# Adding the squares of the new h over its eight tiles on GpSimd, in place of TensorE products in four bands

## The reference

```
def rmsnorm(x, g):
    y = xf * lax.rsqrt(jnp.mean(xf * xf, axis=-1, keepdims=True) + RMS_EPS)
def post_add(h, y, g_post, gate, weight):
    return h + weight * gate[:, None, :] * rmsnorm(y, g_post)

per layer:  h = post_add(h, swiglu(pre_mod(h, ...)), ...)    feed-forward network a
            h = post_add(h, mixer(pre_mod(h, ...)), ...)     attention and gating
            h = post_add(h, swiglu(pre_mod(h, ...)), ...)    feed-forward network b
```

## Time and profile before

| | us |
|---|---|
| median of 3 runs | 2848.84 (2848.16 to 2849.9) |
| profiled execution, its own time | 2847.8 |
| its span | 2846.0 |
| PE busy | 2783.9 (98%) |
| DVE busy | 1298.3 (46%) |
| ACT busy | 971.0 (34%) |
| POOL busy | 111.2 (4%) |

### The profile page before, as it was taken

One profiled execution on the slowest core, in us unless ns is written; L12 is line 12 of the kernel. 1 busy time (PEld: TensorE's weight loads), 2 busy tenths in 40 slices (PEclk: granted clock), 3 DMA queues, 4 the chain that ended last, 5 costly groups with the idle time before them and its releaser, 6 DMA issues.

```text
span 2846.0 us, 49978 instructions
## 1 busy us (share of the span) xinstructions
PE 2783.9 (98%) x21654; PEld 2628.9 (92%) x21654; DVE 1298.3 (46%) x2533; ACT 971.0 (34%) x1821; POOL 111.2 (4%) x210
## 2 busy tenths in 40 slices
PE   7999999999999999999999999999999999999997
PEld 6999999878999989999999999998889999999997
DVE  3444424655544464443264443256555445544423
ACT  4222324444422452222252222244443225422322
POOL 0000000010000000000000000001100000000000
PEclk9999999999999999999999999999999999999999
DMA  6444532333222234432224444323322222222221
GB/s 245 149 148 149 172 121 93 110 123 98 92 82 82 82 104 149 148 134 88 88 86 152 149 149 165 112 100 116 122 96 68 82 82 75 82 82 82 86 87 66
DMA packets 90186, 319.82 MB, mean 112 GB/s; under 512 B 11360, under 2 KB 14464, under 8 KB 89776
## 3 DMA queue, kind: packets, MB, share of 16 engines
q1 hardware_dynamic: 64048, 222.50, 23.4%
q0 software_dynamic: 25920, 94.14, 9.7%
HBM read 305.70 MB, written 11.55 MB: 111 GB/s over the span
## 4 chain that ended last, share of the span: by engine, by line
PE 85%; DVE 7%; ACT 3%; DVEq 2%; issue 2%; DMA 1%; SPq 0%; ACTq 0%
PE ps L668 77%; PE ps L782 2%; PE ps L1013 2%; PE ps L1059 1%; DVE h L1671 1%; ACT w_hi L1162 1%; DVE x_lo L1678 1%; PE ps L1035 1%; DVEq L1670 1%; DVE z L1669 1%; PE ps L677 1%; DMA w_raw<-in_f 1%; ACT sig L1498 1%; ACT x_hi L1254 1%; DVEq L2017 1%
## 5 line engine op out<-in xcount | busy, mean ns | idle before, releaser
L668 PE MATMUL ps<-x_hi,w_hi 128*128 128x290 f32 (+1 forms) x4256 | 973.8, 304 | 22.7 <-DVE x_lo L1678 13.6
L668 PE MATMUL ps<-x_lo,w_hi 128*128 128x290 f32 (+1 forms) x4256 | 935.4, 295 | 0.0
L668 PE MATMUL ps<-x_hi,w_lo 128*128 128x290 f32 (+1 forms) x4256 | 934.8, 295 | 0.0
L668 PEld LDWEIGHTS ps<-x_hi,w_hi 128*128 128x128 f32 x4256 | 686.7, 189 | 95.1 <-issue 65.3
L668 PEld LDWEIGHTS ps<-x_lo,w_hi 128*128 128x128 f32 x4256 | 701.1, 190 | 0.3
L668 PEld LDWEIGHTS ps<-x_hi,w_lo 128*128 128x128 f32 x4256 | 692.7, 189 | 0.0
L1553 DVE TENSOR_TENSOR w_lo<-w_raw,w_hi 128x1024 fp32r<-128x1024 f32 x386 | 468.8, 1222 | 254.2 <-ACT w_hi L1162 251.9
L1162 ACT CAST w_hi<-w_raw 128x1024 fp32r<-128x1024 f32 x386 | 392.9, 1047 | 77.3 <-DMA w_raw<-in_f 77.3
L668 PE MATMUL ps<-hid_hi,w_hi 128*128 128x288 f32 x1344 | 300.8, 295 | 1.8 <-DVE c_col L1610 1.8
L668 PE MATMUL ps<-hid_hi,w_lo 128*128 128x288 f32 x1344 | 300.7, 295 | 0.0
L668 PE MATMUL ps<-hid_lo,w_hi 128*128 128x288 f32 x1344 | 298.7, 293 | 0.0
(11 more groups left out here) (214 smaller groups left out, 2391.8 us busy)
## 6 DMA issues: line engine op xcount, KB each, us to landing
w_raw<-in_f SPq DMA_DIRECT2D x260, 512.0 KB, 3.5
ada_w<-in_ada POOLq DMA_DIRECT2D x128, 512.0 KB, 5.7
w_raw<-in_gate SPq DMA_DIRECT2D x64, 512.0 KB, 3.5
w_raw<-in_tri SPq DMA_DIRECT2D x42, 512.0 KB, 3.5
ada_first<-in_ada SPq DMA_DIRECT2D x4, 2048.0 KB, 17.7
w_raw<-in_wout SPq DMA_DIRECT2D x16, 512.0 KB, 3.4
decay_s<-f_scratch POOLq DMA_DIRECT2D x16, 272.0 KB, 6.0
decay_p<-f_scratch POOLq DMA_DIRECT2D x8, 512.0 KB, 5.9
```

The costliest lines, as they stand in the source:

```text
L668: r = mm(ps[:, 2 * out + b, 0:width], w, xx[:, cols(b)], start=first and n == 0, stop=last and n == 2)
```

## The change

The products in bands and the copy by ACT go away, with their two semaphores. In their place GpSimd adds tiles 1 to 7 of the squares into tile 0, half 0 first, one instruction for a tile and a half: 14 in a boundary, 70 in all. Each waits for its square and for the addition before it. `sum_of_h` keeps its place and now waits for the fourteenth addition. On GpSimd's list the additions of the first boundary of a layer stand behind the loads of network a and ahead of the mixer's DMAs, those of the second ahead of the loads of network b, and those of the third behind them.

```
@@ first_group, on PE
-            some(0, (0, 1, 2), (3, 4, 5))
-            if not first:
-                bands_of_h(*j, 0, 0)
-            some(0, (0, 1, 2), (6, 7))
+            some(0, (0, 1, 2), (3, 4, 5, 6, 7))
...
                 some(1, (0, 1, 2), (k,))
-                if not first and k in LATE_SUMS:
-                    bands_of_h(*j, *LATE_SUMS[k])
@@ sum_of_h, on PE
-            pe.wait_ge(bands_taken.sem, bands_taken.done(l, j))
+            pe.wait_ge(sq_h_added.sem, sq_h_added.done(l, (j + 1) * ADDS - 1))
@@ first_raw and before_pairs, on ACT
-                if s == 1 and (l or ab == "b"):
-                    take_bands(*((l, 1) if ab == "b" else (l - 1, 2)))
...
-                if s == 0:
-                    take_bands(l, 0)
@@ on GpSimd
+        def add_squares(l, j):
+            n = j * ADDS
+            for b in BOTH:
+                total = sq_h[:, 0, columns(b)]
+                for k in range(1, KD):
+                    pool.wait_ge(sq_h_ready.sem, sq_h_ready.done(l, x_index(j, b, k)))
+                    if k > 1:
+                        pool.wait_ge(sq_h_added.sem, sq_h_added.done(l, n - 1))
+                    nc.gpsimd.tensor_tensor(total, total, sq_h[:, k, columns(b)], ALU.add
+                                            ).then_inc(sq_h_added.sem, 1)
+                    n += 1
...
             ada_loads(l, "a")
+            add_squares(l, 0)
             mixer_outputs(l)
...
             stage(l, B_PAIRS + 1, 1, 3, None)
+            add_squares(l, 1)
             ada_loads(l, "b")
+            if l < DEPTH - 1:
+                add_squares(l, 2)
```

More of the change, by code:

```diff
@@ L127 @@
 BAND = P // BANDS
-LATE_SUMS = {1: (0, BANDS), 5: (1, 0), 7: (1, BANDS)}
+ADDS = 2 * (KD - 1)
 BANDS_AT = 2
@@ L487, in build_program @@
     sq_h_ready = S("sq_h_ready", 6 * KD)
-    bands_ready = S("bands_ready", 3)
-    bands_taken = S("bands_taken", 3)
+    sq_h_added = S("sq_h_added", 3 * ADDS)
     sum_h_ready = S("sum_h_ready", 3)
@@ L1210, in first_raw @@
                 r.then_inc(acc_free[s].sem if s < 2 else alt_taken.sem, 1)
-                if s == 1 and (l or ab == "b"):
-                    take_bands(*((l, 1) if ab == "b" else (l - 1, 2)))
-        def take_bands(l, j):
-            act.wait_ge(bands_ready.sem, bands_ready.done(l, j))
-            A(two(sq_h[:, 0, :]), pair[3], ACT.Copy, scale=1.0 / BAND).then_inc(bands_taken.sem, 1)
         def estimate_h(l, j):
```

## The result

| | us |
|---|---|
| before, median of 4 runs | 2848.97 (2848.16 to 2849.9) |
| after, median of 4 runs | 2877.39 (2874.58 to 2879.9) |
| ratio | 1.0099, 95% interval 1.0086 to 1.0111 |
| profiled execution after, its own time and span | 2879.9, 2878.1 |

The change makes the kernel 28.4 us slower; 34.6 us was forecast. The profiled execution is the longest of the four, so its rows show 32 us more than before in place of 28.

The account below looks back on a forecast made before the run. PE, busy 98% of the span, was taken as the bound, waiting for DVE at boundaries. Profiled 2847.8 + 36.0 - 1.4 = 2882.4, with the median 1.0 higher: 2883.4 us; the forecast's own range 2862 to 2897.

Parts of the forecast that it names:

- DVE's chain sets a boundary, and PE moves with it: At both tiles 6 PE already waits for DVE's low part of x, so 7.20 us a boundary delays everything after.
- Each addition holds DVE up for its whole length, 0.65 us: At boundaries, GpSimd additions stall DVE instructions reading two SBUF tiles; 0.65 us each, bounds 0.456 and 1.18; forecast's chance 0.52.
- Rival 1: At the boundaries GpSimd and DVE don't disturb each other; only the 1.4 us saving remains, 2847.4 us; chance 0.28.
- Eleven of the fourteen count: Per boundary, eleven additions delay DVE fully, the third mostly fits DVE's 0.60 us gap, half 1's last two cost nothing.
- The removal saves 1.4 us: Only the last of four band groups costs PE: 0.5 us saved at two boundaries, 0.12 us at three.
- The new wait and the moved loads cost nothing: `sum_of_h` has 1.9 us in hand at worst; network b's first two loads stay hidden with 9 us in hand.
- The sum: Whole kernel: 36.0 us for the hold on DVE less 1.4 us for the removed bands.
- Rival 2: At boundaries POOL stands still instead of DVE, making PE 4.4 us late at `sum_of_h`; +22 us, 2871; chance 0.15.

Follow-up runs that it names:

- experiment 2: Kernel before, bands and copy kept, plus 14 GpSimd additions of 128x288 at each boundary that nothing reads: 2873.53 us, ratio 1.0085.
- experiment 7, third run: Kernel before plus 144 GpSimd additions of 128x256 in the feed-forward networks, two a step, waiting for ACT's hid_hi: 2849.95 against 2849.36 us, ratio 1.0001.
- experiment 3: Kernel before plus 14 GpSimd memsets of 288 columns at each boundary, with the additions' waits and signals: 2849.57 us, ratio 1.0001.
- experiment 1: Changed kernel without its 70 GpSimd additions, so the sum of squares lacks tiles 1 to 7: 2848.42 against 2849.49 us, ratio 0.9996.
- the filler: Changed kernel plus unused PE products ahead of waits for x_lo, 22 in half 0, 4 and 10 in half 1: 2873.63 us, ratio 1.0085.

## Why the prediction was right, point by point

- *DVE's chain sets a boundary, and PE moves with it*: right, and shown. The same additions cost 24.0 us there (experiment 2), and 19.5 us of DVE's time cost nothing where DVE waits for PE (experiment 7, third run).
- *Each addition holds DVE up for its whole length, 0.65 us*: the right mechanism, both numbers off. An addition takes 0.79 us at the shortest and 1.10 us on average. Those that hold DVE up do so for 0.52 us on average, and over all 70 it is 0.49 us. Rival 1, no disturbance, falls with experiments 2 and 3. The Trainium skill's page "SBUF — State Buffer", section "Who interferes with whom", names as colliding a DVE instruction with two SBUF inputs and a GpSimd instruction that reads. Additions and copies, memsets, and DVE's instruction on PSUM behave as it says. It adds that the one that comes later stands still until the other is done, and the trace agrees: z, which ran first, kept its 0.75 us while the addition ended 0.66 us after it, and h, which came later, ended some 0.62 us after the addition. The hold is less than the addition's length since the turn is shorter: 0.66 us of 0.79, and DVE's h, 0.76 us by itself, needs only 0.61 us more once the addition has ended, so about 0.15 us of it had passed while it stood waiting. That the 0.65 us charged is almost the turn is chance: it was taken from ACT's pass, as the length of an addition.
- *Eleven of the fourteen count*: right. Twelve additions end ahead of tile 6 of half 1, and eleven of them hold DVE up, by 0.36 to 0.61 us; one, the second and not the third, runs in DVE's gap of 0.61 us. The eleven make 5.45 us, and the gap of 0.23 us ahead of x_lo is used up: 5.2 us, where PE's delay is 5.14. So the mis-sized term is the hold, 0.50 us in place of 0.65: 5 x 5.16 = 25.8 us in place of the 36.0 worked out.
- *The removal saves 1.4 us*: 1.1 us by experiment 1, which is within its interval, and 1.2 us by its rows.
- *The new wait and the moved loads cost nothing*: right. The fourteenth addition ends 2.7 us ahead of the sum, and memsets in the same place of POOL's list cost nothing (experiment 3).
- *Missing from the prediction*: the clock. The longer waits let PE's clock fall to its lower level, and part of the products after them run at half the rate. In the changed kernel's profiled execution the five fourth chunks are 5.93, 5.75, 6.63, 5.96 and 5.97 us late, 30.2 us together. With the filler, at a clock of 1.00, they are 4.72, 5.09, 5.17, 4.71 and 5.10 us late, 24.8 us. So the clock costs 5.4 us in this execution, the longest of four. Of the medians it is about 4 us: 28.4 us for the changed kernel and 24.1 for the filler kernel, each against its own runs of the kernel before.
- *The sum*: 36.0 - 1.4 = 34.6 us was forecast. Shown are 25.8 us for the hold, 1.1 off for the removal and about 4 for the clock, 28.7 against 28.4. The hold was put 10 us too high and the clock left out, so two errors partly cancel, and that much of the forecast's nearness is luck. The time without the clock's share, 24 us above before, would also lie between 2862 and 2897. In the profiled execution the terms are 25.8 - 1.1 + 5.4 = 30.1 of 32.1 us; the other 2.0 us are not assigned.
- *Rival 2, POOL alone stands still*: it has a part, since POOL stands still too where DVE came first; the mean addition is 0.31 us above the shortest. POOL nevertheless finished in time, and PE never waited for it.

What stays open is which part of an instruction is its turn, and so which of two that begin almost together goes first. At 500.20 us an x_lo began 0.01 us ahead of an addition and yet was the one that stood still, for 0.61 us.

No version beats the kernel before. Experiment 1, which does no adding at all, is its bound in this order of work: taking the bands off PE wins 1.1 us at most, which is not told apart from nothing.

## What to carry to other kernels

An engine that is 4% busy is not free, and no busy share shows it: look for a neighbour's instructions of one form that have become longer while their count stayed. Before work goes to it, ask which instructions of its neighbours will run beside it, what they read, and whether the critical engine waits for them. Ask also what the removed work costs today; here three of four groups of products lay in waits, and the fourth was mostly covered by a copy. A wait that grows can cost twice, by its length and by the lower clock after it.

## What was not expected of the hardware

- GpSimd's additions and DVE's instructions on two SBUF tiles take turns. In 52 of 70 cases the addition of 128x288 ended 0.65 to 0.67 us after the DVE instruction that ran at its start, and in 65 of 70 a DVE instruction ended a fixed time after the addition.
- An addition on GpSimd of 128x288 holds up DVE's instructions on two SBUF tiles by 0.49 us on average, one of 128x144 by 0.21 us, a copy of 128x288 by 0.15 us; a memset by nothing that shows.
- An addition of 128x256 on GpSimd takes 0.73 us beside a DVE instruction on PSUM, and 1.46 us on average beside DVE's on two SBUF tiles.
- PE's granted clock was 0.50 in the stretch from 488 us, after a wait of 3.75 us, and 0.62 in the stretch from 504 us, in which a wait of 1.93 us ends. With products in those waits it stayed at 1.00, and in experiment 2 it was 1.00 in the stretch in which a wait of 1.29 us ends.
